# A diffusion trunk on one core: eight more of the adaLN units computed on VectorE instead of TensorE, in the first MLP's last group and from the gates to the second projection

## What is computed

```python
def adaln(cond, w, b):
    m = jax.nn.silu(cond) @ w + b                  # w: D x 6 D, once for each layer
    return [m[:, j] for j in range(6)]             # shift, scale, gate, twice

def modulate(x, g, shift, scale):
    return rmsnorm(x, g) * (1 + scale) + shift

for l in range(2):
    sh1, sc1, g1, sh2, sc2, g2 = adaln(c, w_ada[l], b_ada[l])     # c_ctx for the context
    h = modulate(x, norm_g[l, 0], sh1, sc1)
    y = neighborhood_attention(h) @ w_o_na  if l == 0  else  gla(h) @ w_o_gla
    x = x + g1 * rmsnorm(y, norm_g[l, 1])
    m = square(relu(modulate(x, norm_g[l, 2], sh2, sc2) @ w1[l])) @ w2[l]
    x = x + g2 * rmsnorm(m, norm_g[l, 3])
```

## Time and profile before

| | us |
|---|---|
| median of 3 runs | 2491.17 |
| lowest, highest | 2489.12, 2491.94 |
| profiled execution, its time | 2489.31 |
| its span, from first to last instruction | 2487.5 |
| TensorE busy | 2434.9 |
| VectorE busy | 1685.1 |
| ScalarE busy | 1087.3 |
| GpSimd busy | 262.6 |

### The profile page before, as it was taken

The page is one execution under the profiler, slowest core; times in us unless marked ns, Lnnn a source line. Parts: engine busy times, 40 slices in busy tenths (PEclk is TensorE's granted clock), DMA queues, the critical chain, the costliest instruction groups (busy, mean ns, idle before and its releaser), DMA issues.

```text
span 2487.5 us, 37359 instructions
## 1 busy us (share of the span) xinstructions
PE 2434.9 (98%) x13794; PEld 1991.1 (80%) x13794; DVE 1685.1 (68%) x2118; ACT 1087.3 (44%) x1495; POOL 262.6 (11%) x465
## 2 busy tenths in 40 slices
PE   6899999999999999999999999999999999999998
PEld 3578888778888888888887877798888888888887
DVE  2246665587767767775568877675888678564665
ACT  3234443464333433333454456585644344343343
POOL 0021111000010010000012144200001001000000
PEclk8999999999999999999999999999999999999999
DMA  9999999969888988987877956659668668666564
GB/s 359 372 289 342 321 322 302 320 225 309 294 278 287 308 284 267 310 281 257 281 251 244 307 171 221 222 190 299 204 226 278 208 220 279 197 200 206 169 207 166
DMA packets 458056, 651.39 MB, mean 262 GB/s; under 512 B 21976, under 2 KB 316696, under 8 KB 456280
## 3 DMA queue, kind: packets, MB, share of 16 engines
q1 hardware_dynamic: 426272, 543.47, 65.6%
q0 software_dynamic: 29312, 105.12, 12.6%
q10 hardware_dynamic: 2360, 1.32, 0.2%
HBM read 634.39 MB, written 15.43 MB: 261 GB/s over the span
## 4 chain that ended last, share of the span: by engine, by line
PE 92%; DMA 3%; DVE 2%; ACT 1%; issue 1%; SPq 0%; DVEq 0%; ACTq 0%
PE PS L1380 24%; PE PS L1461 14%; PE PS L1462 14%; PE PS L1463 14%; PE PS L1383 12%; PE PS L1409 3%; DMA SCR<-in_w_ada 1%; DMA RAW<-in_w_o_na 1%; PE PS L1599 1%; PE PS L1391 1%; PE PS L1393 1%; PE PS L1392 1%; PE PS L1600 1%; PE PS L1601 1%; PE PS L1574 1%
## 5 line engine op out<-in xcount | busy, mean ns | idle before, releaser
L2002 DVE TENSOR_TENSOR WLO<-RAW,WHI 128x1024 fp32r<-128x1024 f32 x740 | 873.6, 1225 | 293.0 <-ACT WHI L1715 242.1
L1380 PE MATMUL PS<-HM,WHI 128*128 128x512 f32 x2560 | 648.4, 395 | 3.0 <-issue 2.6
L1715 ACT ACTIVATE WHI<-RAW 128x1024 fp32r<-128x1024 f32 x370 | 390.2, 1055 | 417.0 <-DMA RAW<-in_w_mlp 163.7
L1380 PEld LDWEIGHTS PS<-HM,WHI 128*128 128x128 f32 x2560 | 459.6, 189 | 101.8 <-issue 15.7
L1461 PE MATMUL PS<-WHI,HID 128*128 128x512 f32 x1152 | 450.5, 391 | 0.0
L1462 PE MATMUL PS<-WLO,HID 128*128 128x512 f32 x1152 | 448.4, 389 | 0.0
L1463 PE MATMUL PS<-WHI,HID 128*128 128x512 f32 x1152 | 448.2, 389 | 0.0
L1719 ACT ACTIVATE WHI<-RAW 128x1024 fp32r<-128x1024 f32 x370 | 388.7, 1051 | 97.4 <-DMA RAW<-in_w_mlp 65.4
L1383 PEld LDWEIGHTS PS<-HM,WLO 128*128 128x128 f32 x2560 | 348.9, 190 | 25.6
L1383 PE MATMUL PS<-HM,WLO 128*128 128x256 f32 x2560 | 356.5, 282 | 0.0
L2075 DVE SCALAR_TENSOR_TENSOR X<-X,CS 128x1024 f32<-128x1024 f32 x240 | 297.0, 1279 | 1.4 <-DMA X<-in_w_ada 0.4
(11 more groups left out here) (260 smaller groups left out, 1994.9 us busy)
## 6 DMA issues: line engine op xcount, KB each, us to landing
RAW<-in_w_mlp SPq DMA_DIRECT2D x512, 512.0 KB, 5.4
ADW<-in_w_ada SPq DMA_DIRECT2D x114, 1024.0 KB, 9.9
X<-in_w_ada POOLq DMA_DIRECT2D x224, 256.0 KB, 3.9
RAW<-in_w_qkv_na SPq DMA_DIRECT2D x68, 512.0 KB, 8.6
RAW<-in_w_qkvg_gla SPq DMA_DIRECT2D x64, 512.0 KB, 5.5
SCR<-in_w_ada SPq DMA_DIRECT2D x16, 1024.0 KB, 11.5
RAW<-in_w_o_na SPq DMA_DIRECT2D x32, 512.0 KB, 7.2
RAW<-in_w_qkvg_gla SPq DMA_DIRECT2D x64, 256.0 KB, 5.0
```

What stands on the lines that cost most here:

```text
L1380: return mm(bank[:, 0:2 * T2], hi[:, k, P * b:P * b + P], act[:, kc, 0:2 * T2], start=first, stop=False)
L1715: actv(WHI[:, 2 * s + u, 0:HALF], RAW[:, u, 0:HALF], ACT.Copy).then_inc(hi_half, 1)
L2002: tt(WLO[:, 2 * s + u, part], RAW[:, u, part], WHI[:, 2 * s + u, part].bitcast(f32), ALU.subtract).then_inc(done, 1)
```

## The change

PU, the number of units in a group of the first MLP on TensorE, goes from 6 to 4: those after part x = 2 of output slabs 0 and 1 are gone in all four groups. Two quads are new, so that there are ten.

- The first, QV − 1, lies in the last group of the first MLP: LAST_UP = 9 tiles in the hidden part, LAST_TILES = 4, 3, 0, 0 in the output slabs; its `quad_rows` is done in output slab 2 behind x = 0.
- The second, QG, has tiles 0 to 2 in gate slabs 3 to 5 (GATES_FROM), tiles 3 and 4 behind the loop of the gates and ahead of `multiply(7)`, and GATE_TILES = 4, 4, 3, 0 (tiles 5 to 8, 9 to 12, 13 to 15) in the second projection; `quad_rows` behind x = 3 of slab 2.

POOL's order changes with it: X returns only behind QG, the gains of norms 1 and 2 are loaded in two parts with the last tiles and X's return between them. Flush 2 now reads the rows of the quad that ACT has just stored, and waits for them (FROM0 + 3 for FROM0 + 2). In a fourth slab `sum_rows` moves from ahead of `gain_y` to behind the two operations of `cross` for x = 0. The squares of x0 and x1 come later for norms 1 and 2.

```diff
-        PU = NB + 2
+        PU = NB
-        QUADS0, QUADS1 = HID_GROUPS - 1, 2
+        QUADS0, QUADS1 = HID_GROUPS, 2
-        SKIP_V = SKIP + 2 * QU
+        SKIP_V = SKIP + 3 * QU
-        FROM1 = QS + 1
+        QG = QS + 1
+        FROM1 = QG + 1
...
+            if f == 1:
+                parts = ("y0", "y1", "x0", "x1", "y2", "x2", "g0", "g1", "x3", "g2")
+            if f == 2:
+                parts = ("y0", "y1", "y2", "x0", "x1", "x2", "g0", "g1", "x3", "g2")
...
-        PLAN_MLP = ((0,), (1,), (), ())
+        PLAN_MLP = ((), (), (), ())
...
-        FLUSHES = [(A_QKV0, 32, A_WO0, 0), (32, 40, 40 - SKIP0, FROM0), (40, 64, 64 - SKIP0 - 2 * QU, FROM0 + 2),
-                   (64, 80, A_WO1, QS), (80, 88, 88 - SKIP_V, FROM1), (88, A_END, A_MLP1, FROM1 + QUADS1)]
+        FLUSHES = [(A_QKV0, 32, A_WO0, 0), (32, 40, 40 - SKIP0, FROM0), (40, 64, A_MLP0 + 3 * PU, FROM0 + 3),
+                   (64, 80, A_WO1, QS + 1), (80, 88, 88 - SKIP_V, FROM1), (88, A_END, A_MLP1, FROM1 + QUADS1)]
...
+        GATES_FROM = {3: 1, 4: 1, 5: 1}
+        LAST_TILES, GATE_TILES = (4, 3, 0, 0), (4, 4, 3, 0)
+        LAST_UP = KC - sum(LAST_TILES)
...
+                for x in range(GATES_FROM.get(r - R_G, 0)):
+                    gate_tile(sum(GATES_FROM.get(q, 0) for q in range(r - R_G)) + x)
...
+            for k in range(3, 5):
+                gate_tile(k)
             multiply(7)
...
-            return_x(FROM1)
             pool.wait_ge(sem("gla_qk_turned"), ITEMS)
             pool.wait_ge(sem("gla_kend"), GLA_H)
             pool.dma_start(GHEAD, g_head_gla[0:1, :].partition_broadcast(P)).then_inc(sem("ghead_in"), 16)
+            set_picks(4, PICKS)
+            for k in range(KC - 4):
+                quad_load(QG, k)
...
-                    if quads is not None and n == YN - 1 and x == 3:
+                    if quads is not None and norm is None and n == YN - 1 and x == 3:
+                        quad_rows(g + quads, 2 * layer + 2)
+                    if quads is not None and norm is not None and n == 2 and x == 0:
+                        pe.wait_ge(mod_done, 3)
                         quad_rows(g + quads, 2 * layer + 2)
...
+                if n == 2 and x == 3:
+                    quad_rows(QG, 4, QUAD0_BANK)
...
-                if flush is not None:
+                if flush is not None and n < YN - 1:
                     sum_rows(flush)
...
                         for x in range(3):
+                            if x == 1 and flush is not None:
+                                sum_rows(flush)
                             for b in range(2):
                                 cross(f, x, b)
...
+            load_gain(1, (0, 1))
             return_x(QV)
-            load_gain(1)
+            load_gain(1, (2, 3))
...
-            load_gain(2)
-            park_x(3, 6)
+            load_gain(2, (0, 1))
+            for k in range(KC - 4, KC):
+                quad_load(QG, k)
+            return_x(FROM1)
+            load_gain(2, (2, 3))
+            park_x(3, 6, None)
```

83 lines of the change are left out of this document (55 added, 28 removed).

## The result

The changed kernel takes 2514.28 us (median of 6 runs, 2510.70 to 2515.07), the kernel before in the same comparison 2490.89. The ratio is 1.0089, 95% interval 1.0079 to 1.0098: slower by 23 us in the medians, beyond the range of 2481 to 2504. The profiled execution has a span of 2513.0 for 2487.5.

A forecast was written before the change was run, and what follows sets the result against it. TensorE, busy 98% of the span, was taken to bound the kernel. Terms: −15.5 + 2.1 − 2.3 + 3.1 + 1.2 + 9.3 + 6.4 = +4.3 on 2491.2, giving 2495.5 us; range 2481 to 2504.

The forecast's parts named there:

- the forecast of +4.3: Whole kernel: sum of all terms in us, give or take 5, added to the median; chance 0.40.
- The units: TensorE: eight units leave at 1.94 us each, -15.5; groups 0 to 2 come 11.6 sooner in all.
- -2.3 forecast: First projection, fourth slab: cross operations run in the idle time while sum_rows waits for rows; bounds 0 and -3.0.
- +0.3 forecast: First MLP's last group and its norm: the predicted total for that stretch in the result's table, in us.
- the term of +3.1: First MLP, last group: flush waits for ACT's stores, and VectorE's tiles overfill output slab 1; bounds 0 and 5.
- +1.2 forecast: Gates: tiles 3 and 4 delay multiply(7), tiles 0 to 2 delay evacuations and SiLU; bound 3.
- +9.3 was forecast for waits: Second projection, slabs 0 to 2: TensorE waits 3.5 behind late tile 12, 5.8 before quad_rows; bounds 3.5 and 13.
- The step behind tile 12: Second projection: four tiles, eight halves, evacuation and gain_y on VectorE take 22.4 us from tile 12's start to tile 15's end.
- a share of 2.5 in a rival: Second projection, rival "cover holds": only VectorE's own sum and the wait for tile 8 remain, 2.5; chance 0.28.
- The rival of transfers: Late tiles in the projection hold VectorE's weight splits; projection 13, whole sum +11.7, 2502.9 us; chance 0.25.
- 384 GB/s asked for: Second projection: weights, units and tiles together ask 192 + 96 + 96 GB/s, where 377 was the most moved.
- +6.4 forecast: Behind second projection's slab 2: X returns 4.6 late, squares of x0 and x1 add 2.5, sum_rows's 0.70 wait goes.

The follow-up runs named there:

- the order alone: Kernel before with only sum_rows moved behind cross(0) in the fourth slab of both projections: 2488.67 us, ratio 0.9988.
- The return alone: Kernel before with only X's return moved into the first MLP's last group, squares of x0 and x1 later: 2494.35 us, ratio 1.0008.
- with the unit away: Changed kernel with the 2 MB units done behind the fourth slabs loaded a slab later in SP's queue: 2516.03 us, ratio 1.0102.
- the run with fillers: Changed kernel with matmuls whose result nobody reads ahead of TensorE's six largest waits: 2516.18 us, ratio 1.0100.
- X's return cut and the unit moved: Kernel with the first new quad alone, unit loaded a slab later, X's return there cut to a sixteenth of its columns: 2486.47 us, ratio 0.9979.
- The kernel with both backlogs away: Changed kernel with units' loads a slab later and the gains' broadcasts for second-projection slabs 0 and 1 cut to a sixteenth: 2506.76 us, single run.

## Why the prediction was wrong

Between the forecast of +4.3 and the +25.4 of the traces lie 21 us: 9.6 in the last group, 6.5 in the second projection, 2.3 behind it, 1.4 at the gates, and 2.0 where the first 150 us were longer, less 0.9 for units that were worth more.

**The units (right).** Groups 0 to 2 give 12.5 us for six units, 2.08 each, with no idle time: 0.14 a unit more than the rows' busy time said.

**First projection (right).** -2.3 forecast, -2.0 in the trace, and the order alone gives it, 1.9 in its trace and some 3 in the medians.

**Last group (wrong, the largest miss: +0.3 forecast, +9.9 measured, 6.9 to 13.1 over the profiles in which it is the same).** The step that failed is the term of +3.1. It priced slabs 0 and 1, ScalarE's wait for the quad's stores and VectorE's tiles. The stores' wait was 1.0, not 2.7, and TensorE stalled in slab 0 not at all, by 0.9 in slab 1. What cost stood in slabs 2 and 3, which the prediction did not walk through: X's 2 MB come back there beside gains, a unit and weights. It priced this return in the second projection and overlooked that the same edit moves the other one too, from behind group 2 to here. The return alone costs 3.0 (2.1 in the medians), and cutting its bytes gives 3.7 to 4.7 back; with tiles, unit and a fuller VectorE beside it the loss is 8 or more, and what each of these adds was not separated.

**Gates (undersized).** +1.2 forecast, +2.6 measured: `turn_out` waits 1.15 and 1.52. The bound was 3.

**Second projection (mechanism right, sizes off).** +9.3 was forecast for waits and +15.8 was lost, 11.4 of it waits. The step behind tile 12 held: 22.4 from its start to tile 15's end, 22.5 measured (1728.42 to 1750.96). Its start was put at 1723 (the 1745.8 for tile 15's end is 22.4 behind 1723.4) and came at 1728.4 though all had begun 0.2 earlier. Landing was taken as 5 to 9 us and was 11.8; and tile 8's wait has no term in the forecast, only a share of 2.5 in a rival. It was 5.90 and stalled TensorE in slab 1 by 3.2. The rival of transfers came nearest: its sign, a tile landing over 6 us after its issue, was there for tile 8 (6.3) and tile 12 (11.8), and it put the projection at 13. Its reason, 384 GB/s asked for, is borne out in part. From 1712 to 1730 the DMA engines were 0.98 busy at 338 GB/s; with the unit away they were 0.69 busy at 212, and the wait was nearly the same. So a full rate isn't needed for it: 1 MB ahead of the tile in its own queue is enough, and so is some 3.5 MB beside it. The Trainium skill, page DMA: Bandwidth & Descriptors, section Specifications, has about 358 GB/s as the limit from HBM to one core, half of what two cores share; 382 was moved in the last group here, so as a cap on one core alone it doesn't hold in this case.

**Behind slab 2 (mechanism right, part missed).** +6.4 forecast, +8.7 measured. X's late return is 4 to 5 of it. Missed was that flush 4, too, now fetches rows of the quad just stored, beside X and four broadcasts in the transfers: the fetch took 7.6 to land and VectorE waited 3.85 for it. This was priced for flush 2 and not here.

**The lower clock.** No term stood for it, and 14.2 us of "rest" are there, 13.4 of them from the last group on. By the run with fillers most of it is no cause of its own: with 6.4 of it gone the time was no shorter.

What stays open is how the 4.1 us split that the last group still lost with X's return cut and the unit moved (1.1 are `quad_rows`); light tiles in that group were not tried. Open, too, is how much of the last 11 us in the projection would go if both waits for tiles did, and how much is VectorE's own sum. The kernel with both backlogs away ran once.

## What to carry to other kernels

An edit that puts a borrowed buffer to use for longer moves the moment at which its old content must come back: find every such transfer, and what else is due in that moment. With two slots, three uses in a row make the third wait for the landing of a load that could only be issued when the first was done; and price a load by what is queued ahead of it at its issue, on its own queue and beside it, not by its median. Two backlogs can hide each other, so that taking away either shows nothing.
